# Issuing the up matrices of a mixture-of-experts stage from ScalarE's DMA queue instead of SyncE's

## The reference, cut to what matters

```python
D_MODEL, MOE_HIDDEN, MOE_EXPERTS, MOE_TOP_K, MOE_BLOCK = 1024, 512, 32, 2, 128

def hier_moe(h, w_group, b_group, w_er, b_er, w_gate, w_up, w_down):
    ...
    def expert_block(args):
        xb, e = args
        return (jax.nn.silu(xb @ w_gate[e]) * (xb @ w_up[e])) @ w_down[e]
    ybuf = lax.map(expert_block, (xbuf.reshape(n_blocks, MOE_BLOCK, d), block_expert)).reshape(-1, d)
    y = jnp.zeros_like(t).at[tok_sorted].add(ybuf[dest] * gate_sorted[:, None])
    return y.reshape(bsz, seq, d)

for layer in range(DEPTH):
    x = x + mixer(rms_norm(x, norm_mix_g[layer]))
    x = x + hier_moe(rms_norm(x, norm_ffn_g[layer]), ...)
```

## Time and profile before

| what | us |
|---|---|
| median of 3 runs | 1731.51 |
| the 3 runs | 1729.74 to 1734.15 |
| the profiled execution | 1726.8 |
| its span, first to last instruction | 1725.0 |
| TensorE busy | 1407.0 |
| ScalarE busy | 246.3 |
| weights and everything else moved | 473.49 MB |

### The profile page before, as it was taken

The page is one execution under the profiler, slowest core; times in us unless marked ns, Lnnn a source line. Parts: engine busy times, 40 slices in busy tenths (PEclk is TensorE's granted clock), DMA queues, the critical chain, the costliest instruction groups (busy, mean ns, idle before and its releaser), DMA issues. The chain is left out here.

```text
span 1725.0 us, 18834 instructions
## 1 busy us (share of the span) xinstructions
PE 1407.0 (82%) x7013; PEld 686.9 (40%) x7013; DVE 539.9 (31%) x1251; ACT 246.3 (14%) x529; POOL 230.0 (13%) x330
## 2 busy tenths in 40 slices
PE   7998746997988878878884988896997887887882
PEld 4444645555333333333332356544433333333330
DVE  6998589123111111110114039524111011011014
ACT  3101222111100000000011027412000000000001
POOL 0007070001111111111100000001111111111110
PEclk9999977996998998998996989996999999899896
DMA  7210502536999999999996110426999999999994
GB/s 241 71 52 21 45 13 84 213 151 236 365 397 411 404 410 412 407 406 409 400 407 248 54 49 2 195 85 228 341 384 410 408 407 406 409 405 411 406 419 160
DMA packets 70724, 473.49 MB, mean 274 GB/s; under 512 B 16676, under 2 KB 23556, under 8 KB 45968
## 3 DMA queue, kind: packets, MB, share of 16 engines
q1 hardware_dynamic: 57872, 448.07, 66.5%
q0 software_dynamic: 11376, 19.83, 3.5%
q10 hardware_dynamic: 1424, 4.89, 0.7%
HBM read 465.92 MB, written 23.59 MB: 284 GB/s over the span
## 5 line engine op out<-in xcount | busy, mean ns | idle before, releaser
L616 PE MATMUL psum<-ring,work 128*64 128x512 f32 x992 | 494.1, 656 | 117.2 <-DMA ring<-in_moe_w_up 115.7
L617 PE MATMUL psum<-ring,work 128*64 128x512 f32 x992 | 494.9, 657 | 0.0
L616 PEld LDWEIGHTS psum<-ring,work 128*64 128x64 f32 x992 | 144.9, 151 | 430.8 <-issue 427.1
L629 PE MATMUL psum<-ring,work 128*64 128x512 f32 x992 | 226.5, 598 | 31.1 <-DVE work L761 31.1
L758 DVE TENSOR_TENSOR work<-work,psum 64x512 f32<-64x512 f32 x64 | 44.2, 690 | 597.2 <-ACT work L722 597.1
L722 ACT ACTIVATE work<-psum 64x512 f32<-64x512 f32 x64 | 37.8, 590 | 833.6 <-PE psum L617 833.6
L617 PEld LDWEIGHTS psum<-ring,work 128*64 128x64 f32 x992 | 144.7, 151 | 2.5 <-issue 1.0
L629 PEld LDWEIGHTS psum<-ring,work 128*64 128x64 f32 x992 | 66.6, 136 | 144.9 <-issue 125.1
L764 DVE COPY work<-psum 128x512 f32<-128x512 f32 x64 | 44.2, 691 | 247.7 <-PE psum L629 247.7
L1562 PE MATMUL psum<-ring,hT 128*128 128x512 f32 x256 | 112.1, 600 | 2.1 <-ACT work L1685 2.1
L902 POOL COPY ints<-ints 64x1 uint32 (+1 forms) x64 | 11.4, 178 | 538.3 <-PE psum L608 499.4
(11 more groups left out here) (362 smaller groups left out, 1450.9 us busy)
## 6 DMA issues: line engine op xcount, KB each, us to landing
ring<-in_moe_w_gate SPq DMA_DIRECT2D x62, 2048.0 KB, 17.5
ring<-in_moe_w_up SPq DMA_DIRECT2D x62, 2048.0 KB, 22.9
ring<-in_moe_w_down SPq DMA_DIRECT2D x62, 2048.0 KB, 23.3
ring<-in_hyb_w_in SPq DMA_DIRECT2D x5, 2048.0 KB, 8.6
work<-y_dram SPq DMA_DIRECT2D x16, 512.0 KB, 7.2
ring<-in_swa_w_qkv SPq DMA_DIRECT2D x3, 2048.0 KB, 15.0
ring<-in_hyb_w_out SPq DMA_DIRECT2D x4, 1024.0 KB, 8.7
h_dram<-work ACTq DMA_DIRECT2D x8, 512.0 KB, 2.6
```

The lines of the kernel that those rows point to most:

```text
L616: nc.tensor.matmul(bank[2 + b][0:BLK, :], XT[b][:, c, :], g[:, c, :], start=c == 0, stop=c == KC - 1)
L617: i = nc.tensor.matmul(bank[2 + b][BLK:P, :], XT[b][:, c, :], u[:, c, :], start=c == 0, stop=c == KC - 1)
L629: i = nc.tensor.matmul(bank[6 + b][BLK * hf:BLK * (hf + 1), :], HTE[b][:, c, :], d[:, c, hf * HALF:(hf + 1) * HALF], start=c == 0, stop=c ...
```

## The change

ScalarE issues the up matrix, right behind its own SiLU; SyncE issues gate and down alone. Experts 0 to 2 and the overflow loop are loaded as before. The functions `wg_v`, `wu_v`, `wd_v` and `load_block_w` only move up in the file, so that `act_moe` can use them; the `dma_start` that was L817 is L731 in the changed kernel.

```diff
         def act_moe(act, l):
@@
-            xe(0, 0)
-            silu(0, 0)
-            xe(1, 1)
-            silu(1, 1)
-            with act.Fori(0, (NE - 2) // 2) as i:
+            def up(e, par):
+                load_block_w(act, e + NE * l, par, 1, w_in[3 * par + 1])
+
+            for e in range(4):
+                xe(e, e % 2)
+                silu(e, e % 2)
+                if e != 2:
+                    up((4, 3, None, 5)[e], e % 2)
+            with act.Fori(0, (NE - 6) // 2) as i:
                 for k in range(2):
-                    xe(i * 2 + 2 + k, k)
-                    silu(i * 2 + 2 + k, k)
+                    xe(i * 2 + 4 + k, k)
+                    silu(i * 2 + 4 + k, k)
+                    up(i * 2 + 6 + k, k)
+            for e in (NE - 2, NE - 1):
+                xe(e, e % 2)
+                silu(e, e % 2)
@@ sp_moe
                     sp.wait_ge(e_gu, b0 + e + 1)
                     load_block_w(sp, e + 2 + NE * l, par, 0, w_in[3 * par])
-                    load_block_w(sp, e + 2 + NE * l, par, 1, w_in[3 * par + 1])
                 rows(e - 1, o, True)
@@
                 sp.wait_ge(e_gu, b0 + used + 1)
                 load_block_w(sp, e + NE * l, par, 0, w_in[3 * par])
-                load_block_w(sp, e + NE * l, par, 1, w_in[3 * par + 1])
```

More of the change, by code:

```diff
@@ L722, in act_silu, with load_block_w @@
             nc.scalar.activation(AA[b], bank[2 + b][0:BLK, :], ACT.Silu).then_inc(done, 1)
+        wg_v = A["moe_w_gate"].rearrange("l e (p c) n -> (l e) p (c n)", c=KC)
+        wu_v = A["moe_w_up"].rearrange("l e (p c) n -> (l e) p (c n)", c=KC)
+        wd_v = A["moe_w_down"].rearrange("l e (p c) n -> (l e) p (c n)", c=HC)
+        def load_block_w(q, le, b, which, done):
+            src = (wg_v, wu_v, wd_v)[which]
+            v = src[bass.ds(le, 1), :, :].rearrange("a p n -> (a p) n") if not isinstance(le, int) else src[le]
+            q.dma_start(W(3 * b + which), v).then_inc(done, 16)
         def act_moe(act, l):
@@ L808, in dve_moe @@
             overflow_blocks(dve, l, body)
[L810 to L817, removed]
         def sp_moe(sp, l, free_s5, free_2, free_0, free_1, next_loads):
```

## The result

| | before | changed |
|---|---|---|
| median, us (8 runs each) | 1730.11 | 1737.22 |
| lowest to highest | 1725.93 to 1734.15 | 1732.43 to 1744.27 |
| profiled execution, its span | 1726.8, 1725.0 | 1732.98, 1731.1 |

The ratio is 1.0041, with a 95% interval of 1.0021 to 1.0061: **7 us slower**. That is inside the forecast range and in the direction of the sum's +2.4 us, but three times its size, and beyond the 0.3% that the forecast still called no change.

A forecast was written before the change was run, and what follows sets the result against it. It took each layer as bound first by TensorE, then by the DMA engines for about 25 experts. Terms 0 + 0 + 2.4 on 1726.8 gave 1729.2 us; against the median, 1731.5 + 2.4 = 1733.9 us, range 1723 to 1745.

The forecast's parts named there:

- the sum: Whole kernel: the terms 0, 0 and +2.4 us added to the time before, giving 1729.2 profiled, 1733.9 by the median.
- the bytes: 0 us: Saturated stretch of each layer: bytes unchanged and engines never run dry, so it takes as long as before, 0 us.
- rival B: Saturated stretches: a third busy queue hides part of gather and scatter cost; faster, 1711.5 or 1723.5 us; chance 0.15.
- Rival D: Saturated stretches: interleaving two streams of weights costs bandwidth; slower by 40 us, 1771.5 us; chance 0.05.
- The end term: Last experts of each layer: late gate delays `pe_gu(30)` and `pe_gu(31)`; 1.2 us a layer between 0 and 4.9, +2.4 us.
- Rival A: `pe_gu(30)` and `pe_gu(31)`: the favoured up matrix delays both layers' ends by 4.9 us each, 9.8 together, 1741.3 us; chance 0.23.
- The order: Expert loads: queues share engines, up lands after some 12 us instead of 23.3, gate 0 to 4.9 later, TensorE awaits gate.
- rival C: SyncE's and ScalarE's hardware queues: no sharing, up still lands after 23 us; the same time, 1731.5 us; chance 0.07.
- ScalarE's issue: Between SiLU and the copy `xe(e+1)`: a 0.38 us issue fits under 0.98 us of cover, so 0 us.

The follow-up runs named there:

- its control: Kernel before with SyncE's last five and ScalarE's last six steps written out of their loops, SyncE issuing every up matrix: 1728.97 us, ratio 0.9990.
- the light pair: Kernel before and changed kernel, each with half of the gate and up product left out, all loads kept: 1711.30 and 1715.62 us.
- the version without the end: Changed kernel with the up matrices of experts 28 to 31 given back to SyncE: 1733.85 us, ratio 1.0034 to the kernel before.
- the repeat: The changed kernel measured once more, nothing altered, with its own profile: 1738.66 us against 1729.43 for the kernel before, ratio 1.0051.
- the version with the last four alone: Kernel before with ScalarE issuing only the up matrices of experts 28 to 31, measured twice: 1731.85 us (ratio 1.0023) and 1734.85 us (1.0013).
- the written-out version: Changed kernel with the last steps written out of their loops, ScalarE issuing every up matrix from 3 on: 1738.29 us, ratio 1.0041.
- the pairs without gathers: Kernel before and changed kernel with the gathers left out: 1666.22 and 1666.88 us; the same for the light pair: 1641.83 and 1642.34 us.

## Why the prediction was right and wrong

**The step that failed is "the bytes: 0 us".** Its premise held: the engines never ran dry, the share is 1.01 in every window of the saturated stretches. But full engines don't move a fixed number of bytes. Over 505 to 885 and 1300 to 1670 us, the three profiles of the changed kernel read 406, 403, 405, 405, 406 and 405 GB/s, a mean of 405.0, where the kernel before and its control read 408 four times. 3 in 408 of the 800 us of both stretches of the earlier trace rows are **5.9 us**, and the packets have 6 us; the light pair measured 4.3 with 1 us of end in it, and the version without the end 4.4. The prediction had seen the row: 1.4 us of an expert's 16.1 went with transfers whose bytes are worth 0.6. It took the other 0.8 as given, and gave rival B the chance that a third queue hides some of it. It should have asked what they hang on. They hang on gathers being in flight (without them rate and packets are alike in both orders), and with the change a gather stays 3 us longer, which is the likely reason that it costs more.

**Rival D was the mechanism in kind, not in cause or size.** It was given 0.05 and priced at a doubling, 40 us; about a seventh of that came, and only beside gathers. Rival B was the wrong way round.

**The end term was right in place, and in size partly by luck.** Predicted 1.2 us a layer between 0 and 4.9; the six layer ends of the changed kernel's three profiles give 1.79, 0.25, 1.47, 1.74, 1.83 and 0.25, a mean of 1.22, or 1.1 above the kernel before: **2.2 us** for both layers, against 2.4. But the steps to it were not as forecast:

- The sum left out its own floor. Lateness can't be under 0, so a shift spread evenly from 0 to 4.9, with 2.5 saved in every other case, makes 1.5 a layer, 3.0 for both and not 2.4.
- `pe_gu(30)` was shifted by more than 2.45 us. Counted from the layer's first SiLU it starts at 456.3 to 459.5 us in the six ends, against 451.3 to 454.8 in the four of the kernel before and its control: 3.7 later by the mean. Part of that was given back at the higher clock, and part by a last landing that itself came 0.6 us later a layer.
- The gate that made TensorE late was not always that of 30. In three of the six ends (layer 0 of the first profile, both layers of the repeat) TensorE stood 6.4 to 7.4 us for the gate of **29**, on the lower clock, and then did the steps of 30 and 31 without a stand for a weight; the gate of 30 had landed over 4 us before its step.
- The profiled executions are short ones: 1732.98 and 1733.39 us, where the medians are 1737.22 and 1738.29. The repeat's, nearer its median, has 3.2 us of end. And the version with the last four alone cost +2.4 and +3.9 by the medians. So the end may be worth more than 2.2.

Rival A is real too, as an extreme that one kernel nearly showed, not as the usual case.

**Sum**: 5.9 + 2.2 is 8.1, or with the 3.3 that the light pair leaves for the rate 5.5; measured were +7.1 and +9.2, and for the written-out version +7.3 against the kernel before and +9.3 against the control (1738.29 less 1728.97), with intervals of 3 to 4 us each way. So the two pieces are of the size of the result, with a few microseconds open. The profiles don't close the sum either. From first SiLU to last landing, both layers together, the three of the changed kernel are only 1.3 us above the two of the kernel before and its control (937.2, 937.8, 939.2 against 934.8, 938.9); and another 2.6 us of their longer spans lie between the stages, from the last SiLU of layer 0 to the first of layer 1 (313.6, 315.4, 313.8 against 311.5, 311.8), where neither piece has anything to add. In the pairs without gathers this part is 3.1 us shorter once and 2.9 longer once, so it may be chance; its cause is open.

That the result lies inside the stated range, and even inside the forecast's own 1729 to 1739, is therefore luck in good part: most of the 7 us belong to a term that the sum had at 0.

**The order** went as written. Hardware queues share the engines (rival C is out): gate and up of one expert, issued together into idle queues at 422.84 and 422.85 us, landed at 436.04 and 436.26, where they had landed 5 us apart. Up lands after 15.2 us by the median, not 12; that first pair took 13.4.

**ScalarE's issue** cost nothing, as predicted: 0.37 us under a cover of 0.97.

The rule of the Trainium skill ("DMA: Bandwidth & Descriptors", section "Issuing engines are not separate DMA queues") would have had the change at 0. That the queues interleave is what the traces show. That nothing but issue time is at stake is not: the change cost 7 us here, and none of it was issue time.

## What to carry to other kernels

A DMA share of 1.0 says that the engines are full, not that the time is bytes over a fixed rate: look for windows in which the rate dips at full share, find the transfer that is under way in them, and ask of every change whether it makes that transfer last longer. A second queue doesn't add bandwidth; it changes who waits, and it favours the queue with the shorter backlog, so what is needed first would belong there (not tried here). Where TensorE's chain and the last landing meet within 0.2 us, as they did here, a late gate up to three experts ahead can come through to the end.

## What the runs showed of the hardware that was not expected

- A gather of token rows (0.13 MB, 0.3 us of transfer at 428 GB/s) costs about 1.0 us beside a full stream of weights: leaving out 64 of them saved 63.9 us of the full kernel (1730.1 to 1666.22) and 69.5 of the light one (on two chips). While its packets move the rate falls from 426 to 353 GB/s at an unchanged share, and the 16 KB packets of the weights take 752 ns in place of 612. With a scatter the rate is 423 GB/s. What makes the gather dear, its reads of HBM, its writes to 64 partitions or its skipped rows, was not tried.
- Two streams of weights of 2 MB each on two hardware queues are moved as fast as one: 428 GB/s in both.
- With a second stream of weights beside them, the small transfers take longer: gathers from 8.8 to 11.8 us, scatters from 8.2 to 9.8.
